# A chunked RWKV-7 scan: the triangle's inverse multiplied into keys and values once per unit

## The reference

```python
def step(state, inp):
    r_t, k_t, v_t, w_t, kk_t, b_t = inp
    sa = jnp.einsum('bhvk,bhk->bhv', state, -kk_t)
    state = (state * w_t[:, :, None, :] + sa[..., None] * b_t[:, :, None, :]
             + v_t[..., None] * k_t[:, :, None, :])
    return state, jnp.einsum('bhvk,bhk->bhv', state, r_t)

s_final, ys = lax.scan(step, s0.astype(jnp.float32), seq)
```

## Time and profile before

| | |
|---|---|
| runs shown, median | 1225.67 us |
| profiled execution, its own time | 1223.6 us |
| its span, first to last instruction | 1221.9 us |
| TensorE busy | 926.2 us (76%) |
| weight loads (beside TensorE) | 574.8 us (47%) |
| VectorE busy | 607.4 us (50%) |
| ScalarE busy | 286.8 us (23%) |
| mean granted TensorE clock | 0.809 of 2.4 GHz |

### The profile page before, as it was taken

How to read it: one execution, slowest core, us unless ns; L and a number is a source line. 1 busy time by engine, 2 the same in 40 slices (tenths; PEclk the granted TensorE clock), 3 DMA queues, 4 the chain that set the end, 5 groups by cost and what they waited for, 6 DMA issues and landing times.

```text
span 1221.9 us, 15392 instructions
## 1 busy us (share of the span) xinstructions
PE 926.2 (76%) x5899; PEld 574.8 (47%) x5899; DVE 607.4 (50%) x1286; ACT 286.8 (23%) x496; POOL 63.3 (5%) x55
## 2 busy tenths in 40 slices
PE   1699997999747788687676968896279987779654
PEld 1355655666446475566555743443234333224221
DVE  2326999455656867678776244534722111012006
ACT  2240000050533505417322143101011111001002
POOL 0000000001001000010010000001011111010000
PEclk9999998999757566575575698897579999889878
DMA  9845522111011101110112427410579999899533
GB/s 329 294 178 214 208 91 73 46 35 27 1 18 27 19 1 27 19 27 1 18 27 53 168 100 247 174 67 34 226 282 420 419 419 419 318 416 421 207 139 135
DMA packets 72744, 193.76 MB, mean 159 GB/s; under 512 B 42309, under 2 KB 42815, under 8 KB 58463
## 3 DMA queue, kind: packets, MB, share of 16 engines
q1 hardware_dynamic: 64416, 174.19, 38.1%
q0 software_dynamic: 5472, 10.53, 2.3%
q10 hardware_dynamic: 2783, 8.06, 1.8%
HBM read 181.80 MB, written 19.34 MB: 165 GB/s over the span
## 4 chain that ended last, share of the span: by engine, by line
PE 45%; DVE 28%; DMA 16%; ACT 5%; issue 4%; SPq 1%; ACTq 0%; DVEq 0%; POOLq 0%; POOL 0%
PE bank L544 8%; DMA arena<-in_expert_w_up 8%; PE bank L2106 8%; DVE arena L947 7%; PE bank L1518 4%; PE bank L2128 3%; PE bank L1231 3%; DVE arena L1035 2%; PE bank L1282 2%; PE bank L1250 1%; PE bank L1253 1%; DVE arena L1084 1%; DVE arena L1082 1%; PE bank L1187 1%; DMA arena<-winv 1%
## 5 line engine op out<-in xcount | busy, mean ns | idle before, releaser
L544 PE MATMUL bank<-arena 128*128 128x320 f32 x704 | 201.3, 446 | 12.2 <-DVE arena L436 3.8
L544 PEld LDWEIGHTS bank<-arena 128*128 128x128 f32 x704 | 135.8, 195 | 79.3 <-issue 28.0
L2106 PE MATMUL bank<-arena 128*64 128x512 f32 (+2 forms) x528 | 130.2, 651 | 32.2 <-DMA arena<-in_expert_w_up 31.3
L947 DVE SCALAR_TENSOR_TENSOR arena<-arena 128x655 f32<-128x655 f32 x116 | 104.6, 902 | 4.6 <-DVE arena L947 0.2
L2106 PEld LDWEIGHTS bank<-arena 128*64 128x64 f32 (+2 forms) x528 | 46.4, 149 | 114.5 <-issue 113.2
L2186 DVE TENSOR_TENSOR arena<-arena,bank 128x256 f32<-128x256 f32 x17 | 7.2, 422 | 158.0 <-ACT arena L2160 158.0
L2128 PE MATMUL bank<-arena 128*64 128x512 f32 (+2 forms) x264 | 65.8, 641 | 10.0 <-DVE arena L2189 10.0
L1518 PE MATMUL bank<-arena 128*128 128x512 f32 x160 | 73.2, 616 | 0.0
L907 ACT ACTIVATE arena<-bank 64x128 f32<-64x128 f32 (+1 forms) x68 | 19.9, 292 | 174.2 <-PE bank L1282 172.8
L1273 PE MATMUL bank<-arena 64*64 64x64 f32 x320 | 25.3, 300 | 42.2 <-DVE arena L1132 34.4
L1518 PEld LDWEIGHTS bank<-arena 128*128 128x128 f32 x160 | 31.2, 197 | 38.8 <-issue 38.8
(11 more groups left out here) (333 smaller groups left out, 1395.5 us busy)
## 6 DMA issues: line engine op xcount, KB each, us to landing
arena<-in_expert_w_gate SPq DMA_DIRECT2D x33, 1024.0 KB, 15.5
arena<-in_expert_w_up SPq DMA_DIRECT2D x33, 1024.0 KB, 19.6
arena<-in_expert_w_down SPq DMA_DIRECT2D x33, 1024.0 KB, 19.3
arena<-in_ada_w SPq DMA_DIRECT2D x12, 2048.0 KB, 10.4
arena<-in_w_in SPq DMA_DIRECT2D x22, 512.0 KB, 3.6
arena<-expert_rows SPq DMA_DIRECT2D x10, 512.0 KB, 7.3
arena<-in_x_sample SPq DMA_DIRECT2D x8, 512.0 KB, 5.9
arena<-in_w_out SPq DMA_DIRECT2D x1, 4096.0 KB, 14.8
```

The costliest lines, as they stand in the source:

```text
L544: mm = nc.tensor.matmul(psum[4 + 2 * (n % 2) + half][:, 0:HALF], wring[:, n % NWIN, k], hT[:, k, half * HALF:(half + 1) * HALF], start=(k ...
L947: chain(nc.vector.scalar_tensor_tensor(acc, src, w, acc, ALU.mult, ALU.add))
L2106: mm = nc.tensor.matmul(psum[2 + n % 2][r, :], xeT[:, n % 2, c, r], gu[:, :, c, :], start=(c == 0), stop=(c == KD - 1))
```

## The change

T leaves the chain. The inverse in GM is multiplied once per unit into both parts of what it used to be applied to: `tv` takes inverse times SAV (the value part, after mv), and `w` takes inverse times keys with decay, for which `turn_a` transposes these keys into a new buffer AT; the result is written over AR's columns 0 to 63. X then gives the removals less their value part, and VectorE's sum writes SAV in place (XS goes, SL gets its own room). Y and S both wait for that sum. The copies of y and z move from VectorE to ScalarE. Events are split into halves or quarters (lora, scan, norm, kp, ar, bk, bonus, turn, mv, the inverse in ten parts instead of five), and nearly all places are new. Cut to its core, without the other splits, whose bodies are unchanged:

```diff
-        EARLY = ["shift_r", "shift_k", "shift_v", "lora_w", "lora_a", "square", "scan", "norm", "exp", "kn", "kp"]
+        EARLY = ["shift_r", "shift_k", "shift_v", "lora_w0", "lora_w1", "lora_a0", "lora_a1", "square", "scan0", "scan1",
+                 "norm0", "norm1", "logn", "exp", "kn", "kp0", "kp1", "kp2"]
+        FILL += [f"{name}{q}" for name in ("turn_bk", "turn_v", "mv", "turn_a") for q in range(4)]
+        INVERT += ["invstore", "place", "ta0", "ta1", "merge_y0", "merge_y1", "merge_z0", "merge_z1"]
+        INVERT += ["tv0", "tv1", "tv2", "tv3", "w0", "w1"]
...
+            "inv0": (0.3498, -0.1143, 0.3644, 0.4290, 0.3470),
...
+            "inv9": (0.4850, 0.6591, 0.6054, 0.6828, 0.6798),
...
+            "place": (0.9905, 0.8825, 0.5840, 1.0435, 0.9465),
+            "ta0": (0.9908, 0.8828, 0.5843, 1.0438, 0.9468),
...
+            "merge_z1": (1.0143, 0.9873, 0.9873, 1.0603, 0.9913),
...
+            "exp": (0.4584, 0.7220, 0.7485, 0.7115, 0.6915),
+            "kn": (0.8561, 0.8070, 0.7780, 0.7480, 0.8270),
...
+            "X": (0.3155, 0.3932, -0.0150, 0.8690, 0.5010),
+            "T": (0.8945, 0.5755, 0.5128, 1.1932, 1.0472),
+            "S": (0.9842, 0.9945, 0.6822, 1.2582, 0.9422),
+            "Y": (0.8459, 0.6440, 0.7606, 1.3610, 1.1920),
+            "turn_a0": (0.4014, 0.4174, 0.7932, 0.3434, 0.3804),
...
+            "tv0": (1.0146, 0.9876, 0.9876, 1.0606, 0.9916),
...
+            "w1": (1.0161, 0.9891, 0.9891, 1.0621, 0.9931),
...
+            USES[f"turn_a{_q}"] = [(f"a{_q}", _q)]
+            USES[f"tv{_q}"] = [(f"tv{_q}", (_q + 2) % 4)]
...
-                elif ev == "T":
-                    g, n = step_at(u, i), len(chunks(u, i))
-                    act.wait_ge(s_SA, g + 1)
-                    for h in range(2):
-                        ins_ = nc.scalar.activation(SAV[b][0:64, i::steps(u), C * h:C * h + C],
-                                                    psum[6 + h][0:64, 0:n * C].rearrange("p (n c) -> p n c", c=C),
-                                                    ACT.Copy)
+                elif ev[:-1] in ("mv", "tv"):
+                    q = int(ev[-1])
+                    use = f"m{q}" if ev[0] == "m" else ev
+                    wait_filled(act, u, use)
+                    h, g0 = q // 2, 8 * (q % 2)
+                    chain.announce(nc.scalar.activation(
+                        SAV[b][0:64, g0:g0 + 8, C * h:C * h + C],
+                        psum[BANK[use]][0:64, :].rearrange("p (n c) -> p n c", c=C), ACT.Copy),
+                        s_read[BANK[use]], read_count(u, use))
...
+                elif ev in ("w0", "w1"):
+                    q = int(ev[1])
+                    wait_filled(act, u, ev)
+                    chain.announce(nc.scalar.activation(
+                        AR[b][:, 8 * q:8 * q + 8, 0:C], psum[BANK[ev]][:, :].rearrange("p (g c) -> p g c", c=C),
+                        ACT.Copy), s_read[BANK[ev]], read_count(u, ev))
...
-                elif ev == "merge_y":
-                    for h in range(2):
-                        wait_filled(dve, u, f"y{h}")
-                        chain.announce(nc.vector.tensor_copy(
...
+                    if i == 0:
+                        for q in range(4):
+                            wait_read(dve, u, f"tv{q}")
                     for h in range(2):
+                        sa = SAV[b][0:64, i::steps(u), C * h:C * h + C]
                         ins_ = nc.vector.tensor_tensor(
-                            XS[0:64, 8 * C * h:8 * C * h + n * C].rearrange("p (n c) -> p n c", c=C),
-                            psum[6 + h][0:64, 0:n * C].rearrange("p (n c) -> p n c", c=C),
-                            SAV[b][0:64, i::steps(u), C * h:C * h + C], ALU.add)
+                            sa, psum[6 + h][0:64, 0:n * C].rearrange("p (n c) -> p n c", c=C), sa, ALU.add)
...
+                elif ev[:-1] == "turn_a":
+                    q = int(ev[-1])
+                    pe.wait_ge(s_ar, u + 1)
+                    wait_free(pe, u, f"a{q}")
+                    for n in range(4):
+                        mm = nc.tensor.transpose(psum[BANK[f"a{q}"]][0:64, n * P:(n + 1) * P], AR[b][:, 4 * q + n, 0:C],
+                                                 ident)
+                    mm.then_inc(s_summed, 1)
+                elif ev in ("w0", "w1"):
+                    q = int(ev[1])
+                    for use in ("z0", "z1", f"a{2 * q}", f"a{2 * q + 1}"):
+                        wait_read(pe, u, use)
+                    wait_free(pe, u, ev)
+                    for n in range(8):
+                        gc_ = 8 * q + n
+                        for h in range(2):
+                            mm = nc.tensor.matmul(psum[BANK[ev]][64 * h:64 * h + 64, n * C:(n + 1) * C],
+                                                  AT[0:64, gc_, C * h:C * h + C], GM[b][0:64, GC * h + gc_, 0:C],
+                                                  start=True, stop=True)
+                    mm.then_inc(s_summed, 1)
...
                     if i == 0:
-                        for use in ("z0", "z1", "m2", "m3"):
+                        for use in ("w0", "w1"):
                             wait_read(pe, u, use)
...
-                elif ev == "T":
-                    g = step_at(u, i)
-                    pe.wait_ge(s_XS, g + 1)
-                    for k, gc_ in enumerate(chunks(u, i)):
-                        for h in range(2):
-                            at = 8 * C * h + C * k
-                            mm = nc.tensor.matmul(psum[6 + h][0:64, k * C:(k + 1) * C], GM[b][0:64, GC * h + gc_, 0:C],
-                                                  XS[0:64, at:at + C], start=True, stop=True)
-                    mm.then_inc(s_SA, 1)
...
                 elif ev == "Y":
                     g = step_at(u, i)
+                    pe.wait_ge(s_SAS, g + 1)
...
             pe_mix([("X", LAST, 0)])
             y_mean(0)
             y_mean(1)
-            pe_mix([("T", LAST, 0)])
-            for use in ("z0", "z1"):
+            for use in ("tv2", "tv3", "w0", "w1"):
                 wait_read(pe, LAST, use)
...
-            pe_mix([("T", LAST, 1)])
```

More of the change, by code:

```diff
@@ new lines, in build @@
+            "merge_z0": (1.0140, 0.9870, 0.9870, 1.0600, 0.9910),
+            "merge_z1": (1.0143, 0.9873, 0.9873, 1.0603, 0.9913),
+            "shift_r": (0.3749, 0.3241, 0.3917, 0.2921, 0.3921),
+            "shift_k": (0.0515, 0.3294, 0.4957, 0.2243, 0.2823),
+            "shift_v": (0.5951, 0.6204, 0.7455, 0.5644, 0.5854),
+            "lora_w0": (0.5385, 0.5476, 0.8598, 0.4575, 0.5215),
+            "lora_w1": (0.5388, 0.5479, 0.8601, 0.4578, 0.5218),
+            "lora_a0": (0.5817, 0.5570, 0.6924, 0.4451, 0.4431),
@@ L870, in act_mix @@
                     chain.announce(nc.scalar.activation(EI, CS, ACT.Exp, scale=KAPPA), s_exp, 3 * u + 3)
-                elif ev in ("turn_bk", "turn_v"):
-                    name = "t" if ev == "turn_bk" else "v"
-                    for q in range(4):
+                elif ev[:-1] in ("turn_bk", "turn_v"):
+                    name = "t" if ev[:-1] == "turn_bk" else "v"
+                    for q in (int(ev[-1]),):
                         wait_filled(act, u, f"{name}{q}")
@@ L986, in dve_mix @@
                             chain(ins_)
-                    chain.announce(ins_, s_cs, u + 1)
-                elif ev == "norm":
-                    for h in range(2):
+                    if ev == "scan1":
+                        chain.announce(ins_, s_cs, u + 1)
+                elif ev in ("norm0", "norm1"):
+                    for h in (int(ev[4]),):
                         wait_filled(dve, u, f"n{h}")
@@ L1038, in dve_mix @@
                             s_read[BANK[f"g{q}"]], read_count(u, f"g{q}"))
-                elif ev == "bonus":
-                    for h, part in enumerate(halves(u)):
+                elif ev in ("bonus0", "bonus1"):
+                    for h, part in ((int(ev[5]), halves(u)[int(ev[5])]),):
                         wait_filled(dve, u, f"b{h}")
@@ L1190, in pe_mix @@
                             mm.then_inc(s_summed, 1)
-                elif ev in ("norm", "bonus"):
+                elif ev[:-1] in ("norm", "bonus"):
                     name = ev[0]
                     pe.wait_ge(s_sq if name == "n" else s_rk, u + 1)
-                    for h in range(2):
+                    for h in (int(ev[-1]),):
                         wait_free(pe, u, f"{name}{h}")
@@ L1236, in pe_mix @@
                     pe.wait_ge(s_wcopy, 2 * (u + 1))
                     lo, hi = slice(0, 32), slice(32, 64)
-                    for name in ({"place": "ta", "merge_y": "y", "merge_z": "z"}[ev],):
-                        for h in range(2):
+                    for name in ({"ta": "ta", "merge_y": "y", "merge_z": "z"}[ev[:-1]],):
+                        for h in (int(ev[-1]),):
                             wait_free(pe, u, f"{name}{h}")
```

230 lines of the change are left out of this document (132 added, 98 removed).

## The result

The changed kernel takes 1243.74 us, the median of four runs (1241.1 to 1247.26), against 1226.1 for the kernel before, measured beside it: a ratio of 1.015, 95% interval [1.0134, 1.0166]. That is 17.6 us more, more than twice the 8 that were forecast. Its profiled execution was the longest of the four (1247.26 us, span 1245.6), so its rows hold 3.5 us that the median does not.

A forecast was written before the change was run, and what follows sets the result against it. No engine is saturated: three fixed-order queues take turns, and the step chain doesn't set the period. Terms +6, +0.3, +3.0, +1.7 and -3 sum to +8 on 1223.6, 1231.6; 2.1 above it, 1234 us; range 1201 to 1254.

The forecast's parts named there:

- The side: Whole kernel: the change makes it slower, chance 0.53, against 0.34 for faster and 0.13 for the same.
- the forecast's own range: Whole kernel: 1226 to 1242 around 1234 us, allowing 2 us of error for each of four periods; chance 0.43.
- the walk of the third and fourth period: Third and fourth period between X.0 starts: 88.2 us against 85.2, +3.0, and 78.5 against 76.8, +1.7.
- rival B: w in the five tails: its products don't pair, +3.4 us in each, 17 in all, 1251 us; chance 0.12.
- D: Tail on TensorE: it runs at the full clock and takes half, -9 us in five tails, 1180 us; chance 0.06.
- The last unit: Last unit, from the last X.0 on: two products leave TensorE's queue, -3 us.
- C: Steady periods: the step chain was the bound and the tail is covered, 27 us less, 1199 us; chance 0.25.
- E: Whole kernel: small errors cancel the excess, unit 0's turns at full clock, third period covered, 1225 us; chance 0.14.
- Unit 0: First unit, up to its X.0: about 6 us later, at 364.6 to 367.4 against 360.18.
- First and second period: First two periods between X.0 starts: 83.1 us each against 82.5 and 83.4, +0.3 together.
- The walk of the steady unit: One steady unit, each queue walked in its new order: X of the next unit at 83.1 us.
- 11 us won ahead of the inverse are given back behind it: Steady period: inverse ends 11 us earlier, but landing to next X takes 28.9 us instead of 17.5; period stays.

The follow-up runs named there:

- old_places: The changed kernel's algebra with every event at the place it had in the kernel before; 1268.37 us, 1.0360 of the kernel before.
- tv_pairs: The changed kernel with the tv products written like w, the two heads alternating between output partitions; 1229.16 us, 1.0055 of the kernel before.
- t_early: The changed kernel with step 1's decay ahead of the Gram masks and the bonus reading its banks first; 1240.88 us, 1.0126 of the kernel before.
- turn_a_late: The changed kernel with the product of step 3 ahead of turn_a in TensorE's queue; 1240.29 us, 1.0132 of the kernel before.
- order_only_2: The changed kernel's new order with the old algebra, the triangle product back in each step at repaired places, kn late; 1221.02 us, 0.9964 of the kernel before.
- kn_late: The changed kernel with VectorE's kn behind the sum of step 7; 1243.75 us, 1.0154 of the kernel before.
- pairs_combo: The changed kernel with the edits of tv_pairs, turn_a_late and kn_late together; 1224.0 us, 0.9994 of the kernel before.
- combo_2: pairs_combo plus the VectorE moves of t_early and new TensorE places for step 7's S and Y; 1221.46 us, 0.9968 of the kernel before.
- combo_3: combo_2 with w ahead of tv; 1218.45 us, 0.9931 of the kernel before.

## Why the side was right and the size wrong

The side was right, and 1243.7 lies in the range of 1201 to 1254, but outside the forecast's own range of 1226 to 1242; 8 us were forecast and 17.6 measured. The step that failed is the walk of the third and fourth period, whose terms of +3.0 and +1.7 measured +6.9 and +7.7.

*Held.* Nobody is saturated and the period is not the step chain: in old_places eight shorter steps brought the landing forward by 1 us at most. The bare step fell as said, 3.86 us from X.6 to X.7 in the fourth period (685.29 to 689.15) for 3.6. The inverse ended 48.1 us into the second period for 47.1, place began 57.2 for 56.1, directly behind the exponentials. The tail is 22.4 for 22.3. w is 3.7 for 3.5 and its rival B is out; tv_pairs shows the reason. The tail's clock is 0.50, so D is out. VectorE idles 14.75 us for 14. The last unit gives back 3.9 for 3. C is out: in the fourth period, where place waited for the DMA, landing to X.0 is 25.1 us (690.51 to 715.61), not under 21, and placing never starts before 56. E is out by the time, though its turns of unit 0 did run at the fast clock (1.94 and 2.26 us).

*Mis-sized.* In the profiled executions the span grew by 23.7 us, 15.7 more than the sum said:
- 3.1 lie ahead of anything that the change touches. The first lora product starts at 246.42 in the profile of after and at 243.33 in that of before, behind the same projection. In the fourteen profiles, which run the same projection ahead of it, it starts anywhere from 243.07 to 248.30, so this is the execution and not the change.
- Unit 0: X.0 6.8 later without those 3.1, said 6.
- First and second period: 1.2 and 1.6 over. Inverse +1.0, placing +0.1 more, step 7 another 0.4: small errors of one sign. The decay beside GpSimd is not among them; t_early took it away and the periods stayed.
- Third period 3.8, fourth 6.0 over. This is the step that failed, 9.8 of the 15.7, and it is the one that the prediction called its weakest, "a wait that I missed". The walk of the steady unit had no wait at X.3, because mv and turn_a fitted ahead of it there. For the third and fourth period I corrected that walk by the sizes of single operations and did not walk them again. In the third, 16 shift pieces on ScalarE hold back mv's copies, so turn_a, so X.3: 3.4 us inside the back-substitution. In the fourth, the order is the same and mv was at the slow clock: 3.2. turn_a_late took 3.4 and 3.2 us off these two periods and nothing off the others. The fourth has 2.5 more that I left out: rk in eight pieces (3.08 for 1.54) and the bonus in twelve (3.8 for 2.8) stand ahead of the back-substitution, which starts 25.3 us into the period for 22.5 in the second. That no run tested by itself.
- Last unit: 0.9 less than said.

These are 3.1 + 0.8 + 1.2 + 1.6 + 3.8 + 6.0 - 0.9 = 15.6.

*Wrong in kind, without harm to the number.* I read "11 us won ahead of the inverse are given back behind it" as two separable effects. order_only_2 shows that they are only in part. In the second period the new order had moved the start of placing from 65.9 to 57.2 us, and with the longer step back it stands at 66.4: at the placing, all of the gain hung on the short step. But VectorE still ends the inverse at 52.0 us there, against 59.1 in the kernel before and 48.1 in the changed one. Most of that gain stays and is not used: placing waits in ScalarE's queue behind the exponentials, which end at 63.8 instead of 57.2, and behind T's copy of step 7. What order_only_2 has over the kernel before is its shorter way from the start of placing to X.0 (13.7 us for 17.5), with the copies of y and z on ScalarE and kn out of the way. So in this order the short step pays by bringing the exponentials forward, more than by the inverse. Whether another order would do that for the longer step is open.

## What to carry to other kernels

Moving a product out of a loop pays in full only if the loop step ends last. Check it by where the next stage's input lands, before and after, in the same period: in the old order it landed at 65.9 and 65.3 us. A shorter step can still let an order work that a longer one blocks (placing at 57.2 against 66.4 us). What is then done once per unit goes to the place that does end last, so price it there and make it cheap there first: alternating the output partitions of 64x64 products halved tv from 6.98 to 3.68 us. A period that has other pieces than the steady one must be walked through again in the full queue order, since a queue's wait is not a sum of sizes.

## What the runs showed of the hardware

- A VectorE operation with two SBUF inputs that came beside a GpSimd operation of 3.61 us took 2.17 to 2.27 us instead of 0.29, and ended 0.15 us behind it. In the kernel before, the VectorE operations beside the same scale in the four latent units read a bank, and none was slow.
- The same 64 records of mv took 3.94 us in the first three periods of the changed kernel, at a granted clock of 1.00, and 7.09 in the fourth, at 0.50. In the fourth period they were slow too in t_early, turn_a_late, kn_late and pairs_combo (6.8 to 7.1 us) and fast in tv_pairs, whose queue around mv is that of the changed kernel, and in combo_2 and combo_3 (3.8 to 3.9). So the level that a product meets cannot be read off its neighbours. With a sum queued behind it, the difference of 3.15 us came back as a wait of VectorE of 3.21. Whether it is the same in every execution of one kernel, one trace of each does not show.
